# Attention: the low parts of a head's 1376 columns in one VectorE operation instead of a GpSimd and a VectorE operation

## The chip, the cores and the metric

The kernel runs on one core of a Trainium2 chip. The metric is the device time of one execution in microseconds. The engines are TensorE (PE for its matmuls, PEld for its weight loads), VectorE (DVE), ScalarE (ACT), GpSimd (POOL) and SyncE (SP), which issues the DMAs. Each engine runs its own instruction stream in order; they meet through semaphores.

## The reference

Two layers over 528 tokens (16 meta tokens and 512) of width 1024: a stick-breaking attention layer with a feed-forward part, then an RWKV-7 layer with a feed-forward part. The change lies in the attention, of which this is the core, for each of 16 heads of 64:

```python
z = jnp.einsum('bhtd,bhsd->bhts', qb, kb).astype(jnp.float32) * scale
mask = (s_idx[None, :] < t_idx[:, None]) & (s_idx[None, :] >= pad)
log_beta = jax.nn.log_sigmoid(z)
log_rest = jnp.where(mask, jax.nn.log_sigmoid(-z), 0.0)
later = lax.cumsum(log_rest, axis=3, reverse=True) - log_rest
att = jnp.where(mask, jnp.exp(log_beta + later), 0.0)
outs.append(jnp.einsum('bhts,bhsd->bhtd', att.astype(vb.dtype), vb))
```

The sum over later keys is taken by matmuls with a triangular matrix of ones.

## The kernel before

Everything is fp32. TensorE works on fp32r operands, so a factor that must keep its precision is split into two of them: a high part (a rounded copy, made by ScalarE) and a low part (the value minus its high part). A product then takes a matmul for each part: three for projections (`x_hi*w_hi`, `x_lo*w_hi`, `x_hi*w_lo`), two where the other factor is exact, as the matrix of ones is.

The attention goes through eight pairs of heads. The scores of one head lie in 1376 columns of 128 keys each: 512 columns in the first PSUM bank and 2 x 432 in the next two. `part(t, 0)` names the first 512 columns of a tile, `part(t, 1)` the other 864. The head `hp` = 0 of a pair has its scores in the PSUM tile `psg`, `hp` = 1 in `psx`.

For each head the steps are: VectorE clips the scores (`clip`, L408), ScalarE takes the exponential (L308) and the logarithm (L314), VectorE takes a maximum (`softplus`, L414), and `rest` is there. ScalarE makes its high part `rest_hi` (`rest_high`, L322), in two pieces of 512 and 864 columns. The low part `rest_lo` is made in two pieces too: GpSimd the first 512 columns (L538), VectorE the other 864 (`rest_low`, L419). With both, TensorE adds the sums within a block of keys (`own_block`, L627). VectorE adds up blocks of later keys (`later_keys`, L431), ScalarE makes their high part (`sums_high`, L330), VectorE the low part (`sums_low`, L436), and TensorE adds these (`later_blocks`, L638). ScalarE's exponential (L336) then gives the weights, with which TensorE multiplies the values (L660, L665).

Between these steps TensorE does the q, k and v projections of the next pair (`half`, L576), in pieces that the order written out in `tensor` puts between them. A projection needs its weights split into `w_hi` (ScalarE, L125) and `w_lo` (VectorE, L129). VectorE's order is also written out by hand: after `rest_low` of both heads come `later_keys` and `sums_low` of both, an eviction of a projection (L392), and then `unit_lo(3p + 4)`, the low part of the weights of the k projection, for which the TensorE block `half(3p + 4, 0)` waits. In the last pair there is no next projection, and the attention's output projection (L1219) fills in, in two pieces.

The semaphores of the change are `rlo_near` (raised by GpSimd's piece), `rlo_far` (raised by VectorE's piece) and `rhi_r` (raised by each piece of `rest_hi`, four times a pair). `own_block` waits for both of the first two, `later_keys` for `rlo_far` alone. `rest_low(p, 0)` stands between `softplus(p, 1, 0)` and `softplus(p, 1, 1)`.

Of the kernel before, what the change touches and what calls it, by code (L numbers as in the profile page):

```python
# [7 lines left out]
F32 = mybir.dt.float32  # L8
# [173 lines left out]
PAIRS = H // 2  # L182
# [9 lines left out]
class Attention:  # L192
# [175 lines left out]
    def vector(self, dve):  # L368
        k, b, nc = self.k, self.b, self.k.nc
# [46 lines left out]
        def rest_low(p, hp):  # L416
            n = 4 * p + 2 * hp + 1
            dve.wait_ge(self.rhi_r.h, n + 1)
            nc.vector.tensor_tensor(self.part(b.rest_lo[hp], 1), self.part(b.rest[hp], 1),  # L419
                                    self.part(b.rest_hi[hp], 1).bitcast(F32), ALU.subtract).then_inc(self.rlo_far.h, 1)  # L420

        def later_keys(p, hp):

# [36 lines left out]
        for p in range(PAIRS):  # L460
# [9 lines left out]
            evict(3 * p + 2, 1)  # L470
            softplus(p, 1, 0)
            rest_low(p, 0)
            softplus(p, 1, 1)
            rest_low(p, 1)
            later_keys(p, 0)
            later_keys(p, 1)
# [20 lines left out]
    def gpsimd(self, pool):  # L497
        k, b, nc = self.k, self.b, self.k.nc
        for c in k.psum_free:
            pool.sem_inc(c.h, c.start)  # L500
        nc.gpsimd.memset(k.ident[:], 0.0).then_inc(self.const_r.h, 1)
        nc.gpsimd.memset(k.ones[:], 1.0).then_inc(self.const_r.h, 1)
        nc.gpsimd.memset(k.eps[:, 0:1], RMS_EPS).then_inc(self.const_r.h, 1)
        nc.gpsimd.memset(k.eps[:, 1:2], 1.0).then_inc(self.const_r.h, 1)
        nc.gpsimd.memset(k.eps[:, 2:3], GN_EPS).then_inc(self.const_r.h, 1)
        pool.wait_ge(self.const_r.h, 5)
        nc.gpsimd.affine_select(out=k.ident[:], in_=k.ident[:], compare_op=ALU.not_equal, fill=1.0, base=0,
                                pattern=[[-1, P]], channel_multiplier=1).then_inc(self.const_r.h, 1)
        nc.gpsimd.memset(b.work[0][:], 0.0).then_inc(self.made_r.h, 1)
        nc.gpsimd.memset(b.work[1][:], -1.0).then_inc(self.made_r.h, 1)  # L510
        nc.gpsimd.memset(b.work[2][:], -1.0).then_inc(self.made_r.h, 1)
        nc.gpsimd.memset(b.vtok[:, 4, :], 0.0).then_inc(self.made_r.h, 1)
        nc.gpsimd.memset(b.kk[:, T:5 * P], 0.0).then_inc(self.made_r.h, 1)
        pool.wait_ge(self.made_r.h, 5)
        nc.gpsimd.affine_select(out=b.work[0][:], in_=b.work[0][:], compare_op=ALU.is_gt, fill=MASKED, base=0,
                                pattern=[[1, P]], channel_multiplier=-1).then_inc(self.made_r.h, 1)
        nc.gpsimd.affine_select(out=b.work[1][:], in_=b.work[1][:], compare_op=ALU.is_ge, fill=0.0, base=0,
                                pattern=[[-1, P]], channel_multiplier=1).then_inc(self.made_r.h, 1)
        pool.wait_ge(self.made_r.h, 7)
        pool.wait_ge(self.const_r.h, 6)  # L520
        for n in range(2):
            nc.gpsimd.tensor_copy(b.neg[:, n, :], b.work[0][:])
        nc.gpsimd.tensor_copy(b.tri[:], b.work[1][:])
        nc.gpsimd.tensor_copy(b.minus[:], b.work[2][:])
        nc.gpsimd.tensor_copy(b.ident_r[:], k.ident[:]).then_inc(self.made_r.h, 1)

        pool.wait_ge(self.sq_r.h, 2)
        nc.gpsimd.tensor_tensor(b.acc[:], b.sq[0][:], b.sq[1][:], ALU.add).then_inc(self.acc_r.h, 2)
        for m in range(2, KT - 1):
            pool.wait_ge(self.sq_r.h, m + 1)  # L530
            pool.wait_ge(self.acc_r.h, m)
            nc.gpsimd.tensor_tensor(b.acc[:], b.acc[:], b.sq[m % 2][:], ALU.add).then_inc(self.acc_r.h, 1)

        for p in range(PAIRS):
            for hp in range(2):
                n = 4 * p + 2 * hp
                pool.wait_ge(self.rhi_r.h, n + 1)
                nc.gpsimd.tensor_tensor(self.part(b.rest_lo[hp], 0), self.part(b.rest[hp], 0),  # L538
                                        self.part(b.rest_hi[hp], 0).bitcast(F32), ALU.subtract).then_inc(self.rlo_near.h, 1)

    def begin_out(self, pe, out, i):

        out.wait_weights(pe, i)
        for t in range(KT - 1):
            out.out_part(pe, i, t)
# [10 lines left out]
    def tensor(self, pe, out):  # L556
        k, b, nc = self.k, self.b, self.k.nc
# [62 lines left out]
        def own_block(p, hp):  # L620

            ps = (k.psg, k.psx)[hp]
            pe.wait_ge(self.rlo_near.h, 2 * p + hp + 1)
            pe.wait_ge(self.rlo_far.h, 2 * p + hp + 1)
            for bank, (at, end) in enumerate(zip(BANK_AT, BANK_AT[1:] + [SCORES])):
                for r in (b.rest_hi[hp], b.rest_lo[hp]):
                    mm(ps[:, bank, 0:end - at], b.tri[:], r[:, at:end], start=False, stop=True, skip_group_check=True)  # L627
# [79 lines left out]
        for p in range(PAIRS):  # L707
            fill = p < PAIRS - 1
            z(p)
            half(3 * p + 2, 0)  # L710
            half(3 * p + 2, 1)
            if fill:
                half(3 * p + 3, 0)
            else:
                pe.wait_ge(self.half_r.h, ATT_UNITS)
                self.wait_freed(pe, 3 * p + 2)
                self.begin_out(pe, out, 0)
            own_block(p, 0)
            if fill:
                half(3 * p + 3, 1, range(4))  # L720
            own_block(p, 1)
            if fill:
                half(3 * p + 3, 1, range(4, KT))
            later_blocks(p, 0)
            later_blocks(p, 1)
            if fill:
                half(3 * p + 4, 0, range(2))
            turn_v(p)
            if fill:
                half(3 * p + 4, 0, range(2, KT))  # L730
            else:
                pe.wait_ge(self.att_r.h, 4 * p + 4)
                self.begin_out(pe, out, 1)
            values(p)
            if fill:
                half(3 * p + 4, 1)
# [2049 lines left out]
```

## Time and profile before

| | |
|---|---|
| time, median of 3 runs | 1640.13 us (1637.53 to 1641.57) |
| the profiled execution's own time | 1632.62 us |
| its span | 1630.9 us |
| PE busy | 1562.1 us, 96% of the span |
| PEld busy | 1407.0 us, 86% |
| DVE busy | 835.9 us, 51% |
| ACT busy | 622.9 us, 38% |
| POOL busy | 156.3 us, 10% |
| attention's pairs of heads | from about 38 us to about 276 us of the span |

An engine's busy share says how full it is over the whole span; whether a longer instruction on it costs time depends on who waits for that instruction where it stands. Matmuls are pipelined and their ends are modelled, so the starts of TensorE's rows are the better measure. The mean granted clock of TensorE is 0.983 over the span. Times below are microseconds from the start of the span.

### The profile page before, as it was taken

How to read it: one execution, taken by the hardware profiler on the slowest of the kernel's cores; microseconds unless marked ns; L12 is line 12 of the kernel's file. 1: busy time of each engine (PE TensorE's matmuls, PEld its weight loads, DVE VectorE, ACT ScalarE, POOL GpSimd, SP SyncE). 2: the span in 40 equal slices, each digit the busy share in tenths (PEclk: the TensorE clock that was granted, in tenths of full speed). 3: DMA queues.
4: the chain of work that ended last, by engine and by line, in shares of the span. 5: the costliest groups of instructions: out<-in, count | busy, mean ns of one | idle time of the engine just before them, and what ended most of it. 6: DMA issues, size and time to landing. Idle time of an engine off the chain costs nothing. (4 is left out here: it accounts for less than half of the span.)

```text
span 1630.9 us, 35213 instructions
## 1 busy us (share of the span) xinstructions
PE 1562.1 (96%) x15881; PEld 1407.0 (86%) x15881; DVE 835.9 (51%) x1156; ACT 622.9 (38%) x847; POOL 156.3 (10%) x180
## 2 busy tenths in 40 slices
PE   7999998999999999979999979999789999999997
PEld 6989987999999999979998978888558888888886
DVE  5666765544433444367566545545575444244432
ACT  4655654422212222246567333333344222123322
POOL 3100100011000014000000321101010010001100
PEclk9999999999999999988999989999999999999999
DMA  4122121233332333242222100000313333233331
GB/s 133 53 72 59 53 72 58 80 94 89 104 90 78 91 91 111 74 138 70 74 73 59 39 19 4 4 4 4 107 39 91 90 98 107 88 88 98 101 95 64
DMA packets 214421, 120.63 MB, mean 74 GB/s; under 512 B 8728, under 2 KB 209584, under 8 KB 214016
## 3 DMA queue, kind: packets, MB, share of 16 engines
q1 hardware_dynamic: 213968, 118.31, 24.6%
q8 instruction: 125, 2.05, 0.5%
q14 instruction: 24, 0.20, 0.0%
q10 hardware_dynamic: 304, 0.08, 0.0%
HBM read 111.95 MB, written 6.42 MB: 73 GB/s over the span
## 5 line engine op out<-in xcount | busy, mean ns | idle before, releaser
L125 ACT ACTIVATE w_hi<-w_raw 128x1024 fp32r<-128x1024 f32 (+1 forms) x192 | 213.5, 1112 | 561.5 <-PE psg L785 461.5
L785 PE MATMUL psg<-x_hi,w_hi 128*128 128x264 f32 (+1 forms) x1080 | 350.8, 325 | 1.8 <-DVE w_lo L129 1.8
L785 PE MATMUL psg<-x_lo,w_hi 128*128 128x264 f32 (+1 forms) x1080 | 351.1, 325 | 0.0
L785 PE MATMUL psg<-x_hi,w_lo 128*128 128x264 f32 (+1 forms) x1080 | 350.3, 324 | 0.0
L129 DVE TENSOR_TENSOR w_lo<-w_raw,w_hi 128x1024 fp32r<-128x1024 f32 (+1 forms) x192 | 249.1, 1298 | 130.0 <-ACT w_hi L125 130.0
L785 PEld LDWEIGHTS psg<-x_hi,w_hi 128*128 128x128 f32 x1080 | 203.3, 188 | 20.3 <-DVE w_lo L129 2.2
L785 PEld LDWEIGHTS psg<-x_lo,w_hi 128*128 128x128 f32 x1080 | 203.1, 188 | 17.6 <-issue 0.2
L785 PEld LDWEIGHTS psg<-x_hi,w_lo 128*128 128x128 f32 x1080 | 203.7, 189 | 16.7
L785 PE MATMUL psg<-mid_hi,w_hi 128*128 128x264 f32 (+1 forms) x451 | 145.7, 323 | 0.0
L785 PE MATMUL psg<-mid_lo,w_hi 128*128 128x264 f32 (+1 forms) x451 | 145.6, 323 | 0.0
L785 PE MATMUL psg<-mid_hi,w_lo 128*128 128x264 f32 (+1 forms) x451 | 145.2, 322 | 0.0
L1867 PE MATMUL psg<-x_hi,w_hi 128*128 128x264 f32 x400 | 118.9, 297 | 9.5 <-DVE x_lo L1459 8.2
L959 DVE TENSOR_TENSOR res<-res,psg 128x512 f32<-128x512 f32 (+1 forms) x45 | 31.3, 695 | 173.3 <-PE psg L785 160.7
L1867 PE MATMUL psg<-x_hi,w_lo 128*128 128x264 f32 x400 | 116.7, 292 | 0.0
L1867 PE MATMUL psg<-x_lo,w_hi 128*128 128x264 f32 x400 | 116.6, 292 | 0.0
L1143 POOL TENSOR_TENSOR mid_lo<-up,mid_hi 128x528 fp32r<-128x528 f32 (+1 forms) x40 | 52.6, 1315 | 659.2 <-ACT mid_hi L908 659.2
L985 DVE TENSOR_TENSOR gate<-psg,rstd 128x528 f32<-128x528 f32 (+1 forms) x44 | 30.8, 700 | 122.4 <-PE psg L785 115.4
L1867 PEld LDWEIGHTS psg<-x_hi,w_hi 128*128 128x128 f32 x400 | 78.5, 196 | 14.8 <-issue 11.9
L785 PEld LDWEIGHTS psg<-mid_hi,w_hi 128*128 128x128 f32 x451 | 84.7, 188 | 6.9
L785 PEld LDWEIGHTS psg<-mid_hi,w_lo 128*128 128x128 f32 x451 | 84.8, 188 | 6.7
L785 PEld LDWEIGHTS psg<-mid_lo,w_hi 128*128 128x128 f32 x451 | 84.7, 188 | 6.7
L995 DVE TENSOR_TENSOR up<-psg,rstd 128x528 f32<-128x528 f32 (+1 forms) x44 | 30.8, 700 | 111.7 <-PE psg L785 111.7
(394 smaller groups left out, 3267.1 us busy)
## 6 DMA issues: line engine op xcount, KB each, us to landing
w_raw<-in_w_ffn_in_dram SPq DMA_DIRECT2D x88, 512.0 KB, 3.8
w_raw<-in_w_ffn_out_dram SPq DMA_DIRECT2D x32, 704.0 KB, 4.6
w_raw<-in_w_qkv_dram SPq DMA_DIRECT2D x24, 512.0 KB, 3.8
w_raw<-in_w_rkv_dram SPq DMA_DIRECT2D x24, 512.0 KB, 4.1
w_raw<-in_w_o_attn_dram SPq DMA_DIRECT2D x8, 512.0 KB, 4.0
w_raw<-in_w_o_rwkv_dram SPq DMA_DIRECT2D x8, 512.0 KB, 4.2
v_first<-v_pair SPq DMA_DIRECT2D x8, 264.0 KB, 2.0
res_kept<-res SPq DMA_DIRECT2D x1, 2112.0 KB, 7.8
```

What stands on the lines that cost most here:

```text
L125: k.nc.scalar.activation(k.w_hi[j][:, 0:kt, :], k.raw[j][:, 0:kt, :], ACT.Copy).then_inc(k.hi_ready[j].h, 1)
L129: k.nc.vector.tensor_tensor(k.w_lo[j][:, 0:kt, :], k.raw[j][:, 0:kt, :], k.w_hi[j][:, 0:kt, :].bitcast(F32), ALU.subtract).then_inc(k.lo_r ...
L785: done = k.nc.tensor.matmul(k.psg[:, 2 * j + c, 0:size], w[:, t, :], x, start=t == first and n == 0, stop=t == last and n == 2)
L959: nc.vector.tensor_tensor(row, row, self.psum(i % 2), ALU.add).then_inc(self.freed(i), 1)
L985: nc.vector.tensor_tensor(self.cols(b.gate), self.psum(0), self.cols(k.rstd), ALU.mult)\
L995: nc.vector.tensor_tensor(self.cols(b.up), self.psum(1), self.cols(k.rstd), ALU.mult)\
L1143: nc.gpsimd.tensor_tensor(b.mid_lo[:, r, self.t0:T], b.up[:, self.t0:T], b.mid_hi[:, r, self.t0:T].bitcast(F32), ALU.subtract).then_inc(se ...
L1867: done = nc.tensor.matmul(k.psg[:, 2 * j + c, 0:size], w[:, t, :], x[:, at:at + size], start=t == 0 and a == 0, stop=t == KT - 1 and a == 2)
```

## The change

VectorE makes the low parts of all 1376 columns of a head in one instruction. GpSimd's two instructions a pair are gone, and with them the semaphore wait of TensorE for them; the wait for `rlo_far` stays. The names `rlo_near` and its semaphore are left without use.

```diff
         def rest_low(p, hp):
             n = 4 * p + 2 * hp + 1
             dve.wait_ge(self.rhi_r.h, n + 1)
-            nc.vector.tensor_tensor(self.part(b.rest_lo[hp], 1), self.part(b.rest[hp], 1),
-                                    self.part(b.rest_hi[hp], 1).bitcast(F32), ALU.subtract).then_inc(self.rlo_far.h, 1)
+            nc.vector.tensor_tensor(b.rest_lo[hp][:], b.rest[hp][:], b.rest_hi[hp][:].bitcast(F32), ALU.subtract)\
+                .then_inc(self.rlo_far.h, 1)
...
-        for p in range(PAIRS):
-            for hp in range(2):
-                n = 4 * p + 2 * hp
-                pool.wait_ge(self.rhi_r.h, n + 1)
-                nc.gpsimd.tensor_tensor(self.part(b.rest_lo[hp], 0), self.part(b.rest[hp], 0),
-                                        self.part(b.rest_hi[hp], 0).bitcast(F32), ALU.subtract).then_inc(self.rlo_near.h, 1)
...
         def own_block(p, hp):

             ps = (k.psg, k.psx)[hp]
-            pe.wait_ge(self.rlo_near.h, 2 * p + hp + 1)
             pe.wait_ge(self.rlo_far.h, 2 * p + hp + 1)
```

On VectorE, in the first pair, the order of the instructions around the change is this (`rest_67`, `rest_hi_69`, `rest_lo_71` are those of head 0, `rest_68`, `rest_hi_70`, `rest_lo_72` those of head 1; what an instruction waits for stands in brackets):

```order
 L400 TENSOR_TENSOR v_pair<-psx,rstd 128x264 [waits unit_done0]
 L414 TENSOR_TENSOR rest_68<-rest_68,psx 128x512 [waits a_ln]
-L419 TENSOR_TENSOR rest_lo_71<-rest_67,rest_hi_69 128x864 [waits a_rest_hi]
+L419 TENSOR_TENSOR rest_lo_71<-rest_67,rest_hi_69 128x1376 [waits a_rest_hi]
 L414 TENSOR_TENSOR rest_68<-rest_68,psx 128x864 [waits a_ln]
-L419 TENSOR_TENSOR rest_lo_72<-rest_68,rest_hi_70 128x864 [waits a_rest_hi]
+L419 TENSOR_TENSOR rest_lo_72<-rest_68,rest_hi_70 128x1376 [waits a_rest_hi]
 L431 TENSOR_TENSOR rest_67<-rest_67 128x16 [waits a_lo_far]
 L431 TENSOR_TENSOR rest_67<-rest_67 128x144 [waits a_summed]
```

Nothing changes its place there; two instructions a pair grow from 864 to 1376 columns.

## Rows read from the trace of the kernel before

**Rows 1.** Windows view, one pair of heads: busy time and granted clock by engine.
```profile
core 0: us, PE busy (x) PEld busy (x) DVE busy (x) ACT busy (x) POOL busy (x), PEclk, DMA share, GB/s
128.00:158.00 30.00, 29.84 (x238) 27.16 (x237) 19.79 (x31) 16.82 (x23) 2.60 (x2) 1.00 0.21 63
```

**Rows 2.** Source view of L617, the last matmuls of a pair's scores.
```profile
L617 PE MATMUL psg<-neg,ident_r x8: 363/364/364, 38.0 to 248.0; 128*128 128x256 f32 x8
```

**Rows 3.** Waits of PE and PEld, 38 to 248 us: total, times, longest.
```profile
PE psg L576 <- DVE w_lo L129: 1.0, 6, 0.2
...
PEld psg L576 <- DVE w_lo L129: 1.7, 7, 0.3
```

**Rows 4.** Timeline of VectorE (DVE): start, duration, engine, line, [idle before <-releaser].
```profile
135.17 0.68 DVE L414 TENSOR_TENSOR rest<-rest,psx 128x512 f32<-128x512 f32 x1
135.84 1.06 DVE L419 TENSOR_TENSOR rest_lo<-rest,rest_hi 128x864 fp32r<-128x864 f32 x1
136.81 1.05 DVE L414 TENSOR_TENSOR rest<-rest,psx 128x864 f32<-128x864 f32 x1
138.86 1.06 DVE L419 TENSOR_TENSOR rest_lo<-rest,rest_hi 128x864 fp32r<-128x864 f32 x1 [0.99 <-ACT rest_hi L322]
139.83 1.90 DVE L431 TENSOR_TENSOR rest<-rest 128x16 f32<-128x16 f32 x6
141.81 2.03 DVE L436 TENSOR_TENSOR sum_lo<-rest,sum_hi 128x864 fp32r<-128x864 f32 x2
...
144.10 1.21 DVE L129 TENSOR_TENSOR w_lo<-w_raw,w_hi 128x1024 fp32r<-128x1024 f32 x1
```

**Rows 5.** Timeline of ScalarE (ACT), the same stretch.
```profile
134.90 0.91 ACT L322 ACTIVATE rest_hi<-rest 128x864 fp32r<-128x864 f32 x1
...
137.90 0.93 ACT L322 ACTIVATE rest_hi<-rest 128x864 fp32r<-128x864 f32 x1 [0.67 <-DVE rest L414]
140.85 1.83 ACT L330 ACTIVATE sum_hi<-rest 128x864 fp32r<-128x864 f32 x2 [2.03 <-DVE rest L431]
```

**Rows 6.** Timeline of GpSimd (POOL), the same stretch, second head.
```profile
137.31 1.30 POOL L538 TENSOR_TENSOR rest_lo<-rest,rest_hi 128x512 fp32r<-128x512 f32 x1 [2.36 <-ACT rest_hi L322]
```

**Rows 7.** Timeline of TensorE's weight loads (PEld), first load of four blocks.
```profile
137.40 0.19 PEld L627 LDWEIGHTS psg<-rest_hi,tri 128*128 128x128 f32 x1
...
140.12 0.19 PEld L627 LDWEIGHTS psx<-rest_hi,tri 128*128 128x128 f32 x1
...
142.93 0.19 PEld L638 LDWEIGHTS psg<-sum_hi,minus 128*128 128x128 f32 x1
...
145.37 0.19 PEld L576 LDWEIGHTS psg<-x_hi,w_hi 128*128 128x128 f32 x1 [0.25 <-DVE w_lo L129]
```

**Rows 8.** Groups of VectorE instructions by form: busy us, mean ns of one.
```profile
L129 DVE TENSOR_TENSOR w_lo<-w_raw,w_hi 128x1024 fp32r<-128x1024 f32 x160 | 196.9, 1231 | 105.3 <-ACT w_hi L125 105.3
L129 DVE TENSOR_TENSOR w_lo<-w_raw,w_hi 128x1408 fp32r<-128x1408 f32 x32 | 52.1, 1629 | 24.7 <-ACT w_hi L125 24.7
...
L419 DVE TENSOR_TENSOR rest_lo<-rest,rest_hi 128x864 fp32r<-128x864 f32 x16 | 16.9, 1058 | 7.9 <-ACT rest_hi L322 7.9
```

**Rows 9.** The view of rows 8, and the groups of GpSimd.
```profile
L378 DVE SCALAR_TENSOR_TENSOR x_lo<-res,vec,x_hi 128x528 fp32r<-128x528 f32 x8 | 8.9, 1131 | 0.0
L414 DVE TENSOR_TENSOR rest<-rest,psx 128x864 f32<-128x864 f32 x8 | 8.4, 1048 | 0.0
...
L408 DVE TENSOR_SCALAR rest<-psx 128x864 f32<-128x864 f32 x8 | 8.4, 1047 | 0.0
...
L943 DVE SCALAR_TENSOR_TENSOR x_lo<-res,vec,x_hi 128x528 fp32r<-128x528 f32 x8 | 6.1, 762 | 0.0
...
L532 POOL TENSOR_TENSOR x_acc<-x_acc,x_sq 128x528 f32<-128x528 f32 x5 | 8.7, 1732 | 2.0 <-ACT x_sq L296 1.4
```

**Rows 10.** Timelines of VectorE and of the weight loads, the last pair.
```profile
261.84 2.03 DVE L436 TENSOR_TENSOR sum_lo<-rest,sum_hi 128x864 fp32r<-128x864 f32 x2
...
262.95 0.19 PEld L638 LDWEIGHTS psg<-sum_hi,minus 128*128 128x128 f32 x1
```

## The prediction

> **What bounds the kernel now.** The windows view of one pair of heads comes first [rows 1]. In 30 us TensorE is busy 29.84 us, VectorE 19.79 us and GpSimd 2.60 us, at a granted clock of 1.00, the 2.4 GHz level. Read alone, this says that VectorE has a third of its time free and that two instructions there could grow at no cost. But a share tells nothing about place. The source view of L617, which a pair's scores end with, gives the period: eight starts from 38.0 to 248.0 us, so 210.0 / 7 = 30.0 us a pair [rows 2]. The question is then which wait TensorE ends last within a period. The view of waits has one releaser for its projections here, `w_lo` on VectorE (L129): seven times on the weight loads, 1.7 us in all, and six times on the matmuls, 1.0 us [rows 3]. The waits are small, some 0.24 us each, but they come once in each of the seven pairs that have a next projection. A wait that TensorE meets in every pair, however short, means that up to this point VectorE has no slack left: what VectorE gets later, TensorE gets later.
>
> So the last step is to follow VectorE back from that `w_lo`, by the timelines of one pair [rows 4, 5]. `w_lo` runs from 144.10 to 145.31, and TensorE's next load comes at 145.37, 0.06 us after it [rows 7]. In front of it on VectorE stand the two `sums_low` (141.81 to 143.84) and a short eviction, with no wait among them. The first `sums_low` starts as ScalarE's first `sums_high` ends (two of them take 1.83 us from 140.85, so the first ends near 141.77). That one waited for the third addition of `later_keys`, whose six additions run from 139.83 to 141.73, straight behind `rest_low` of head 1 (138.86 to 139.92). That waited 0.99 us for ScalarE's second piece of `rest_hi` (137.90 to 138.83). ScalarE had itself stood idle 0.67 us for `softplus` on VectorE (136.81 to 137.86), and this stood right behind `rest_low` of head 0 (135.84 to 136.90). The chain from 135.84 to 145.37 is therefore one of instructions that each start within 0.1 us of the end of another, with both `rest_low` in it. GpSimd's piece is not in it: it ends at 138.61, 1.31 us ahead of VectorE's piece of the same head [rows 6, 4].
>
> **The change, part by part.** *GpSimd's two instructions a pair go.* Worth nothing by themselves: TensorE waits for near and far together, and the far one came last, at 139.92 against 138.61 [rows 4, 6]. The second wait on TensorE goes with it; it had long been fulfilled. I take 0.
>
> *`rest_low` grows by 512 columns.* The trace has no 1376-column instruction, but it has the same operation on the same kinds of operands (SBUF twice, out in fp32r) at 864 columns with 1058 ns, at 1024 with 1231 ns and at 1408 with 1629 ns [rows 8]. Between the last two a column costs 398 / 384 = 1.036 ns. From 1408 down by 32 columns gives 1596 ns; from 864 up by 512 it gives 1588 ns. I take 1591 ns, so +0.533 us a head. The bounds: the same difference taken between 864 and 1408 gives 571 / 544 x 512 = 0.537 us. If the 512 columns brought a whole instruction's fixed part as well, 1058 - 864 x 1.036 = 163 ns, it would be 0.70 us a head. Below 0.53 no row leads.
>
> *Where it lands.* In head 0, +0.533 moves `softplus(p, 1, 1)`, then ScalarE's `rest_hi` and so the start of `rest_low` of head 1: the 0.99 us and 0.67 us of idle there do not absorb it, since each is a wait for the other engine of the same chain. In head 1 another +0.533 comes on top. From its end on, everything to `w_lo` is +1.066 us a pair. Nothing that TensorE does can absorb it, since TensorE is released by `w_lo`.
>
> *Where TensorE stands instead.* Its `own_block` of head 0 comes at 137.40 [rows 7]; the low part ends at 136.90 + 0.53 = 137.43, a wait of 0.1 us. `own_block` of head 1 comes at 140.12, and was ready at 139.92 + 0.06 = 139.98, so it had 0.14 us of slack. It is now ready at 139.98 + 1.07 = 141.05, and TensorE stands 0.93 us. `later_blocks` came at 142.93 [rows 7], 0.06 us after the first `sums_low` (141.81 + 1.06 = 142.87) [rows 4]: already set by VectorE, so 1.07 late. The wait for `w_lo` keeps its 0.2 us. So the loss is 1.07 us in each of seven pairs, of which 0.93 shows as a new wait at L627 for `rest_lo`, the rest at L638: 7 x 1.066 = 7.5 us.
>
> *The last pair.* Its two `own_block` lie together, after a piece of the output projection, and find their low parts there. `later_blocks` comes at 262.95, and its `sums_low` was done at 261.84 + 1.06 = 262.90 [rows 10]; 262.90 + 0.06 is the time at which it came, so the whole 1.07 us counts again. From there to the end of the attention all runs behind TensorE.
>
> *After the attention* nothing has changed, and all is moved by the sum. 7.5 + 1.07 = **8.5 us**. Against the profiled execution: 1632.6 + 8.5 = 1641.1 us, span 1639.4. That execution was 7.5 us below the median of the runs shown; on the median the same sum gives 1640.1 + 8.5 = **1648.6 us**.
>
> **Weighed against the skill.** GpSimd's piece could cost more than it seems, by slowing VectorE: VectorE's `x_lo` of 528 columns takes 1131 ns on average at L378, where GpSimd adds up squares for the same norm (L532), and 762 ns at L943, where it doesn't [rows 9]. The Trainium skill (SBUF — State Buffer, section "SBUF: two separate sides") says that a VectorE operation with two SBUF inputs and a GpSimd operation that reads SBUF shut each other out for a whole instruction. By that rule the pairs gain nothing from a free GpSimd, since `softplus` reads one input from PSUM and one from SBUF, and the sum stays at 8.5 us; the trace agrees with its 1048 ns. If the rule's lock held for `softplus` as well, the time would be that of rival 3.
>
> **The rivals.**
> 1. *Half of it is absorbed* (+4.3 us, 1644.4). The idle time of VectorE before `rest_low` of head 1, 0.99 us, is more than the 0.53 us that the first head adds [rows 4]. If that time were slack, only the second head's growth would reach TensorE: 8 x 0.533 = 4.3 us, 0.26%. Against it: ScalarE's idle 0.67 us in front of `rest_hi` ends with `softplus` [rows 5], which moves by the whole 0.53.
> 2. *More than the instructions* (+11 us and beyond). Either each grown instruction costs the 0.70 us bound, 16 x 0.70 = 11.2 us, 1651.3; or the new gap of 0.9 us on TensorE in each pair lowers the granted clock. Against the clock: it is 1.00 over the pair [rows 1], with its waits. If it fell to its 1.2 GHz level for 1 us of matmuls in each pair, that would add 1 us a pair, 1656.6.
> 3. *The freed port, and a faster kernel.* Place: VectorE's `softplus` beside GpSimd's piece, once a head. If each of them had been shut out up to the length of GpSimd's instruction, 1.30 us [rows 6], the change would give back 2.6 us a pair against 1.07 lost: 8 x (1.07 - 2.60) = -12.3 us, 1627.8. It decides from 1.07 us given back in a pair on. Against it: `softplus` of head 1 (136.81 to 137.86) lies half beside GpSimd (from 137.31) and takes 1048 ns, where the clip of the same width takes 1047 ns with GpSimd idle [rows 4, 6, 9].
> 4. *The share of VectorE is what counts, and nothing moves* (1640.1): VectorE has 10.2 us free in each pair [rows 1]. The waits for `w_lo` in all seven pairs speak against it [rows 3].
>
> **How the numbers follow.** A measurement of this kernel tells about 0.3%, 4.9 us, from no change. The forecast, a loss between 7.4 us (8 x 0.93, if only the new wait counted) and 9.5 us, has 0.83; a larger loss by rival 2 has 0.07. Rival 1 has 0.05, rival 4 has 0.03 and rival 3 has 0.02. So slower by over 0.3% is 0.90, within it 0.08, faster 0.02. The range reaches down to rival 1 with the scatter of the runs shown (1644.4 - 0.9 = 1643.5) and up to the 0.70 us bound with the same (1651.3 + 1.2 = 1652.5).
>
> **What would show it.** Right: `rest_low` at 128x1376 with 1591 ns; the starts of L617 some 31.07 us apart instead of 30.0; a new wait of TensorE at L627 for `rest_lo` on L419 of about 0.9 us, seven times, and none in the last pair; `w_lo` still the releaser at L576 with about 0.2 us; `softplus` unchanged at 1047 ns; the last matmul of the attention 8.5 us later, and everything after it as before. Wrong: a period of 30.5 us (rival 1), a granted clock below 1.00 between 38 and 285 us (rival 2), `softplus` clearly shorter (rival 3), or L627 without a wait (rival 4). The surest way to be wrong outside of this is a difference between executions in the 1350 us behind the attention, which the change does not touch.

## The result, and the profile after

The changed kernel's median was 1653.32 us over 8 executions (1643.94 to 1661.46), that of the kernel before 1641.46 us over 8. The ratio is 1.0073 with a 95% interval of 1.0045 to 1.0101: slower by 0.7%, 7 to 17 us. (A ratio here is not the quotient of the two medians beside it; three of the executions that follow, each over 1.5% above the fastest of its set, are in the medians and counts and are left out of ratios and means.) The forecast was slower by 8.5 us, 1648.6 us, in a range of 1643.5 to 1652.5 us. The direction was right and the size lies in the interval, but the median fell 0.8 us outside the range. The profiled execution took 1647.89 us, with a span of 1646.2 us, 15.3 us longer than that of before: 1.5 us of it lie ahead of the first pair's scores, 7.5 in seven pairs, 2.6 from the last pair's scores to the end of the output projection, and 3.6 behind it. So there are two questions: does the attention cost what the sum said, and where is the rest?

First the attention. The windows view of one pair, 31.07 us from scores to scores (busy time and count for each engine, granted clock, DMA), answers to [rows 1]:

```profile
core 0: us, PE busy (x) PEld busy (x) DVE busy (x) ACT busy (x) POOL busy (x), PEclk, DMA share, GB/s
132.72:163.79 31.07, 30.34 (x237) 27.25 (x237) 20.87 (x31) 16.82 (x23) 0.00 (x0) 1.00 0.20 60
```

TensorE's busy time rises by only 0.5 us of the 1.07 us, and VectorE's by 1.08 us. The source view of the last matmuls of the scores (now L610) gives the period, (257.0 - 39.5) / 7 = 31.07 us, against 30.0 in [rows 2]:

```profile
L610 PE MATMUL psg<-neg,ident_r x8: 364/364/364, 39.5 to 257.0; 128*128 128x256 f32 x8
```

The waits of TensorE and of its weight loads between 38 and 260 us (total, times, longest), against [rows 3]:

```profile
PE psx L619 <- DVE rest_lo L419: 4.0, 7, 0.6
PE psg L569 <- DVE w_lo L129: 1.1, 7, 0.2
...
PEld psx L619 <- DVE rest_lo L419: 5.5, 7, 0.8
...
PEld psg L569 <- DVE w_lo L129: 1.7, 7, 0.3
PEld psg L630 <- DVE sum_lo L436: 1.4, 7, 0.2
```

The wait for `w_lo` has stayed what it was, 1.7 us in seven times. In front of it stand two new ones: 5.5 us for `rest_lo`, seven times 0.79 us, and 1.4 us for `sum_lo`, seven times 0.2 us. In the last pair (the same view between 260 and 330 us) TensorE doesn't wait for `rest_lo`, as forecast, and the whole delay shows at `later_blocks`; the kernel before has no such wait there:

```profile
PEld psg L630 <- DVE sum_lo L436: 1.2, 1, 1.2
```

VectorE in the fourth pair, against [rows 4]:

```profile
140.58 1.59 DVE L419 TENSOR_TENSOR rest_lo<-rest,rest_hi 128x1376 fp32r<-128x1376 f32 x1
142.09 1.05 DVE L414 TENSOR_TENSOR rest<-rest,psx 128x864 f32<-128x864 f32 x1
144.13 1.59 DVE L419 TENSOR_TENSOR rest_lo<-rest,rest_hi 128x1376 fp32r<-128x1376 f32 x1 [0.99 <-ACT rest_hi L322]
145.64 1.90 DVE L431 TENSOR_TENSOR rest<-rest 128x16 f32<-128x16 f32 x6
147.62 2.03 DVE L436 TENSOR_TENSOR sum_lo<-rest,sum_hi 128x864 fp32r<-128x864 f32 x2
...
149.91 1.22 DVE L129 TENSOR_TENSOR w_lo<-w_raw,w_hi 128x1024 fp32r<-128x1024 f32 x1
```

ScalarE beside it, against [rows 5]:

```profile
143.17 0.93 ACT L322 ACTIVATE rest_hi<-rest 128x864 fp32r<-128x864 f32 x1 [1.20 <-DVE rest L414]
146.66 1.84 ACT L330 ACTIVATE sum_hi<-rest 128x864 fp32r<-128x864 f32 x2 [2.56 <-DVE rest L431]
```

And the first weight loads of three blocks, against [rows 7]:

```profile
145.78 0.19 PEld L619 LDWEIGHTS psx<-rest_hi,tri 128*128 128x128 f32 x1 [0.79 <-DVE rest_lo L419]
...
148.74 0.19 PEld L630 LDWEIGHTS psg<-sum_hi,minus 128*128 128x128 f32 x1 [0.21 <-DVE sum_lo L436]
...
151.18 0.19 PEld L569 LDWEIGHTS psg<-x_hi,w_hi 128*128 128x128 f32 x1 [0.24 <-DVE w_lo L129]
```

VectorE's idle time in front of the second `rest_low` is still 0.99 us: the first `rest_low` ended 0.53 us later, and with it the softplus, ScalarE's `rest_hi` (idle 1.20 us instead of 0.67) and the start of the second. From the end of the second on all is 1.07 us late. The groups by form (busy us, mean ns of one), against [rows 8, 9]:

```profile
L419 DVE TENSOR_TENSOR rest_lo<-rest,rest_hi 128x1376 fp32r<-128x1376 f32 x16 | 25.5, 1592 | 8.0 <-ACT rest_hi L322 7.9
...
L408 DVE TENSOR_SCALAR rest<-psx 128x864 f32<-128x864 f32 x8 | 8.4, 1048 | 0.0
...
L414 DVE TENSOR_TENSOR rest<-rest,psx 128x864 f32<-128x864 f32 x8 | 8.4, 1048 | 0.0
```

The operation of 1376 columns takes 1592 ns (forecast 1591), and the softplus still 1048 ns without GpSimd beside it.

### The profile page after: what moved, and what is told of

Its sections match the earlier page's. It is cut to its first block and busy times, and to the rows that moved or that the text cites. A ratio compares the mean times of both kernels' runs of the same rounds, so it can differ in the third digit from the quotient of the medians.

```text
span 1646.2 us, 35181 instructions
## 1 busy us (share of the span) xinstructions
PE 1570.2 (95%) x15881; PEld 1412.6 (86%) x15881; DVE 844.9 (51%) x1156; ACT 622.8 (38%) x847; POOL 134.0 (8%) x164
```

## The experiments

All kernels are compared with executions of the kernel before on the same chip. Besides the total, three things are read from each trace: the period of a pair; the **last pair**, from the start of the last scores' last matmul (the 248.0 of [rows 2]) to the start of a fixed matmul after the attention (at 314.9 us in the kernel before, the last that reads `o_hi` or `o_lo`); and a **stretch of the RWKV stage**, between the starts of two fixed matmuls, numbers 7400 and 14070 of the 15881 (counted from 0; 950.4 and 1207.8 us in the kernel before). No kernel here changes anything in that stretch.

| kernel | period, us | last pair | RWKV stretch | median (n) | before, same chip (n) | ratio, 95% interval |
|---|---|---|---|---|---|---|
| before | 30.01 | 66.92 | 257.4 | | | |
| changed | 31.08 | 69.55 | 262.4 | 1653.3 (8) | 1641.5 (8) | 1.0073, 1.0045 to 1.0101 |
| e1_again | 31.09 | 69.51 | 271.6 | 1659.0 (6) | 1643.9 (28) | 1.0107, 1.0075 to 1.0139 |
| e8_again2 | 31.07 | 69.53 | 261.2 | 1652.9 (11) | 1640.5 (34) | 1.0072, 1.0043 to 1.0102 |
| e11_again3 | 31.07 | 67.99 | 261.5 | 1651.9 (12) | 1643.0 (29) | 1.0052, 1.0029 to 1.0075 |
| e2_gaps | 30.0 | 68.43 | 260.4 | 1643.5 (12) | 1643.9 (28) | 1.0001, 0.9974 to 1.0029 |
| e3_head0 | 30.56 | 67.47 | 264.8 | 1649.2 (12) | 1643.9 (28) | 1.0033, 1.0011 to 1.0056 |
| e4_nopool | 30.01 | 66.93 | 261.8 | 1642.2 (12) | 1640.5 (34) | 1.0013, 0.9983 to 1.0042 |
| e5_once | 30.01 | 66.93 | 264.4 | 1650.8 (11) | 1643.9 (28) | 1.0065, 1.0033 to 1.0096 |
| e6_evict | 29.68 | 68.43 | 271.7 | 1638.1 (12) | 1640.5 (34) | 0.9989, 0.9963 to 1.0014 |
| e7_after_evict | 30.75 | 68.03 | 261.1 | 1647.4 (12) | 1640.5 (34) | 1.0036, 1.0007 to 1.0065 |
| e9_last | 30.01 | 67.99 | 264.4 | 1643.6 (12) | 1643.0 (29) | 1.0017, 0.9986 to 1.0047 |
| e10_notlast | 31.07 | 66.94 | 258.1 | 1652.8 (12) | 1643.0 (29) | 1.0070, 1.0040 to 1.0100 |

### Once more, and a delay in one piece (e1_again, e5_once)

The changed kernel was run again as it was:

> The changed kernel once more, unchanged, for the part of the result that the sum doesn't hold. Both theories: the period of a pair in the trace is 31.07 us against 30.0. Theory 1 (the change costs the 8.5 us of the attention, and the rest of the measured difference is scatter of the clock in the stages behind it): the median lies between 5 and 12 us above the kernel before on the same chip, and TensorE's time at its lower clock level comes in other places than in the first trace of the changed kernel. Theory 2 (the gaps in the attention make the clock fall more often behind it, a cost of its own of 3 to 4 us): again 11 to 13 us above, with a stretch at the lower level right behind the attention, near 291 us, as in the first trace.

Its median was 15.1 us above the kernel before, beyond both ranges, with only 6 executions (1655.3 to 1668.7). The period was as both said. A stretch of 3.4 us at the lower clock level came near 290 us again, as theory 2 had it; but the largest difference was in the RWKV stage. The windows view of that stretch, of the kernel before, of the changed kernel (with the time right behind its attention) and of this execution:

```profile
core 0: us, PE busy (x), PEclk, DMA share, GB/s
950.40:1207.80 257.40, 232.64 (x6684) 0.98 0.06 20
```

```profile
288.00:298.00 10.00, 8.26 (x55) 0.83 0.36 105
962.30:1224.70 262.40, 236.94 (x6682) 0.96 0.06 20
```

```profile
964.60:1236.20 271.60, 245.36 (x6687) 0.92 0.06 19
```

The same 6670 matmuls take 257.4 us at a granted clock of 0.98, 262.4 us at 0.96 and 271.6 us at 0.92, where 1.00 is 2.4 GHz and 0.5 is the lower level, 1.2 GHz. The kernel before had, in its one profiled execution, the least time of all thirteen traces.

In e5_once the loss was put in one piece ahead of the pairs:

```diff
         dve.wait_ge(self.rs_r.h, 2)
+        late = self.first_r
+        for n in range(7):
+            if n:
+                dve.wait_ge(late.h, n + 1)
+            nc.vector.tensor_tensor(b.rest[1][:, 0:2 * T], flat(k.res[:, 0:2, :]), flat(k.res[:, 2:4, :]), ALU.add)\
+                .then_inc(late.h, 1)
+        dve.wait_ge(late.h, 8)
         evict(0, 0)
```

> The kernel before with seven additions of 1056 columns on VectorE (unused results) in front of the first eviction of q: one delay of 8.3 to 8.9 us ahead of the attention's pairs instead of a small one in each pair. The pairs keep their period of 30.0 us. Theory 1 (scatter behind the attention): like the changed kernel, some 8.5 us more than before, and no difference between this kernel and the changed one that can be told. Theory 2 (the small gaps lower the clock later): 8.5 us here, and the changed kernel 3 to 4 us above it.

It missed in two ways. The seven additions came every 1.29 us, 9.0 us in all. And TensorE, which stood waiting for most of it, was at the lower level there, as the window shows (the same columns):

```profile
34.00:48.00 14.00, 4.10 (x16) 0.51 0.24 68
```

Up to 1073 us its trace runs about 11 us behind that of before; 9.0 of it is the additions, and 1.9 us arise between 34 and 37 us of the kernel before, in this window. Its median was 6.9 us above, its mean (1653.6 us) 10.3 us above that of all executions of the kernel before (1643.3 us). So it doesn't separate the theories as planned: it shows that the total of a kernel with a known delay scatters by some us around that delay.

### The same work in VectorE's waits (e2_gaps)

```diff
-        def rest_low(p, hp):
-            n = 4 * p + 2 * hp + 1
+        def rest_low(p, hp, which=1):
+            n = 4 * p + 2 * hp + which
...
             softplus(p, 0, 1)
+            rest_low(p, 0, 0)
             evict(3 * p + 2, 1)
             softplus(p, 1, 0)
             rest_low(p, 0)
             softplus(p, 1, 1)
+            rest_low(p, 1, 0)
             rest_low(p, 1)
```

`rest_low` handles the 512 or the 864 columns again, both on VectorE, and TensorE waits for both. GpSimd does nothing, as in the changed kernel.

> VectorE does all of the low parts as in the changed kernel, but the 512 columns of each head as an operation of their own, of some 0.69 us, in a place where VectorE waits anyway: in front of the second eviction of v (0.66 us idle) and behind the last softplus (0.99 us idle). Theory 1 (only the place on the chain to w_lo costs): a period of 30.0 us and the time of the kernel before, within 2 us. Rival (VectorE's added work costs wherever it stands): 2 x 0.6 us a pair, a period of 31.2 us and 9 to 10 us more than before.

VectorE in one pair:

```profile
139.19 1.04 DVE L414 TENSOR_TENSOR rest<-rest,psg 128x864 f32<-128x864 f32 x1
140.15 0.68 DVE L419 TENSOR_TENSOR rest_lo<-rest,rest_hi 128x512 fp32r<-128x512 f32 x1
140.90 0.43 DVE L400 TENSOR_TENSOR v_pair<-psx,rstd 128x264 f32<-128x264 f32 x1
...
141.92 1.06 DVE L419 TENSOR_TENSOR rest_lo<-rest,rest_hi 128x864 fp32r<-128x864 f32 x1
142.90 1.05 DVE L414 TENSOR_TENSOR rest<-rest,psx 128x864 f32<-128x864 f32 x1
143.86 0.68 DVE L419 TENSOR_TENSOR rest_lo<-rest,rest_hi 128x512 fp32r<-128x512 f32 x1
144.94 1.06 DVE L419 TENSOR_TENSOR rest_lo<-rest,rest_hi 128x864 fp32r<-128x864 f32 x1 [0.39 <-ACT rest_hi L322]
```

The two operations of 0.68 us lie in the gaps: the eviction at 140.90 comes as early after the softplus as before, and the idle time in front of the last `rest_low` has shrunk from 0.99 to 0.39 us. The period is 30.0 us and the ratio 1.0001. VectorE does more work here than in the changed kernel, 684 + 1058 - 1592 = 150 ns a head, and it costs nothing. The rival falls: the change's cost is where the work stands, not how much it is. (The edit splits the operation and moves one part of it; the two were not tried apart.) The average period over all pairs is 30.4 us only because the first pair ran at the lower level, as the windows show; from the second pair on there is no such stretch:

```profile
core 0: us, PE busy (x), PEclk, DMA share, GB/s
34.00:48.00 14.00, 13.19 (x60) 0.51 0.26 76
74.03:254.06 180.03, 179.08 (x1412) 1.00 0.21 63
```

### Head 0 alone (e3_head0)

```diff
+            whole = slice(0, SCORES) if hp == 0 else slice(512, SCORES)
+            nc.vector.tensor_tensor(b.rest_lo[hp][:, whole], b.rest[hp][:, whole],
+                                    b.rest_hi[hp][:, whole].bitcast(F32), ALU.subtract).then_inc(self.rlo_far.h, 1)
...
-            for hp in range(2):
+            for hp in (1,):
```

TensorE's wait for GpSimd's piece stays for head 1 alone.

> The change for head 0 alone; head 1 keeps GpSimd's piece. Theory 1 (the growth of head 0's operation passes through softplus and ScalarE's rest_hi undiminished): a period of 30.53 us, 4.3 us more than before, and TensorE waits some 0.4 us a pair at the second own_block. Rival 1 of the prediction (the 0.99 us idle before rest_low of head 1 absorbs it): a period of 30.0 us and no more time than before.

```profile
139.22 1.59 DVE L420 TENSOR_TENSOR rest_lo<-rest,rest_hi 128x1376 fp32r<-128x1376 f32 x1
140.73 1.05 DVE L414 TENSOR_TENSOR rest<-rest,psx 128x864 f32<-128x864 f32 x1
142.77 1.06 DVE L420 TENSOR_TENSOR rest_lo<-rest,rest_hi 128x864 fp32r<-128x864 f32 x1 [0.99 <-ACT rest_hi L322]
```

The 1.59 us of head 0 moves the softplus, and the 0.99 us idle in front of head 1's operation is undiminished. The period is 30.56 us, +0.55; the last pair +0.55. The median was 5.3 us above before. The prediction's first rival falls. TensorE's wait at the second `own_block` is 0.2 us, five times, in the view of its matmuls; its weight loads stand idle there 2.3 us in seven times, 0.33 us each, near the 0.4 us expected.

### GpSimd left out, VectorE as before (e4_nopool)

```diff
-        for p in range(PAIRS):
-            for hp in range(2):
-                n = 4 * p + 2 * hp
-                pool.wait_ge(self.rhi_r.h, n + 1)
-                nc.gpsimd.tensor_tensor(self.part(b.rest_lo[hp], 0), self.part(b.rest[hp], 0),
-                                        self.part(b.rest_hi[hp], 0).bitcast(F32), ALU.subtract).then_inc(self.rlo_near.h, 1)
+        pool.wait_ge(self.acc_r.h, KT - 1)
+        for hp in range(2):
+            nc.gpsimd.tensor_scalar(self.part(b.rest_lo[hp], 0), b.acc[:, 0:512].rearrange("p (a b) -> p a b", b=512), 0.0, None, ALU.mult)\
+                .then_inc(self.rlo_near.h, 1)
...
-            pe.wait_ge(self.rlo_near.h, 2 * p + hp + 1)
+            if p == 0:
+                pe.wait_ge(self.rlo_near.h, hp + 1)
```

> The kernel before without GpSimd's sixteen operations and without TensorE's wait for them; VectorE keeps its 864 columns. The low parts of each head's first 512 columns are left at zero, set once, so a part of the computation is missing. Theory 1 (GpSimd is off the path, TensorE waited for the far part): period 30.0 us, softplus of 864 columns still 1047 ns, the time of the kernel before within 2 us. Rival 3 of the prediction (GpSimd slows VectorE): a shorter softplus and a period of under 30.0 us.

```profile
L414 DVE TENSOR_TENSOR rest<-rest,psx 128x864 f32<-128x864 f32 x8 | 8.4, 1048 | 0.0
```

Softplus 1048 ns, period 30.01 us, ratio 1.0013 with 1 inside the interval. GpSimd's part was off the path and cost VectorE nothing; the third rival falls.

### An eviction moved into the gap (e6_evict, e7_after_evict)

```diff
             softplus(p, 1, 1)
+            if not last:
+                evict(3 * p + 3, 0)
             rest_low(p, 1)
...
             sums_low(p, 1)
-            if not last:
-                evict(3 * p + 3, 0)
             unit_lo(k, dve, 3 * p + 4, KT)
```

The same edit in the kernel before (e6_evict) and in the changed one (e7_after_evict).

> The kernel before with the eviction of q's first half (0.43 us) moved from in front of w_lo to in front of rest_low of head 1, where VectorE waits 0.99 us. Theory (w_lo is the last to release TensorE in every pair, by 0.24 us): TensorE's waits for w_lo at its projections vanish, the period falls from 30.00 to between 29.75 and 29.85 us, 1 to 2 us less in all, which the timed runs can't tell but the trace can. Rival (the wait for w_lo is only the last of many equal ones): the period stays at 30.0 us.

```profile
137.90 1.05 DVE L414 TENSOR_TENSOR rest<-rest,psx 128x864 f32<-128x864 f32 x1
138.87 0.43 DVE L392 SCALAR_TENSOR_TENSOR q_pair<-psg,rstd 128x264 f32<-128x264 f32 x1
139.95 1.06 DVE L419 TENSOR_TENSOR rest_lo<-rest,rest_hi 128x864 fp32r<-128x864 f32 x1 [0.65 <-ACT rest_hi L322]
...
142.90 2.03 DVE L436 TENSOR_TENSOR sum_lo<-rest,sum_hi 128x864 fp32r<-128x864 f32 x2
144.85 1.22 DVE L129 TENSOR_TENSOR w_lo<-w_raw,w_hi 128x1024 fp32r<-128x1024 f32 x1
```

The eviction lies at 138.87, in the gap, and `w_lo` follows the second `sums_low` directly. TensorE's waits for `w_lo` are gone, and the period is 29.68 us, 0.32 us less: that is nearly all of the 0.34 us that VectorE saves, and more than the 0.15 to 0.25 expected. Matmul for matmul against the kernel before, 0.30 us of it arises at the first one behind `w_lo`, so that wait cost a little more than the 0.24 us that the view of waits gives it. TensorE waits for no other engine in these seven pairs any more. Over seven pairs this is 2.3 us. The total can't show it: ratio 0.9989, 0.9963 to 1.0014. By the trace this is the best of the kernels here.

> The same move in the changed kernel. Theory: it takes 0.34 us off the way to w_lo, but the waits at own_block and at later_blocks stand, so the period falls from 31.07 to about 30.8 us: TensorE is held by later_blocks instead of w_lo, and the kernel is still some 6.8 us slower than before. Rival (only w_lo sets the period): 31.07 - 0.34 = 30.73 us, 6.1 us slower.

```profile
PEld psx L619 <- DVE rest_lo L419: 5.5, 7, 0.8
...
PEld psg L630 <- DVE sum_lo L436: 1.4, 7, 0.2
```

The period is 30.75 us, again 0.32 us less; TensorE's waits for `rest_lo` (5.5 us) and `sum_lo` (1.4 us) are as in the changed kernel, the one for `w_lo` is gone. 30.75 lies between the two figures and doesn't choose between them, but the waits do: `w_lo` holds TensorE no more, and `later_blocks` does, as the theory had it. Matmul for matmul against the kernel before, TensorE is 1.04 us late there and 0.76 us late behind `w_lo`. And between these two kernels the change costs 30.75 - 29.68 = 1.07 us a pair again, with no wait for `w_lo` in either: the growth reaches TensorE by `own_block` and `later_blocks` as well. A repair of one place gives back a third of the loss.

### The change in two halves, and more executions (e8_again2, e9_last, e10_notlast, e11_again3)

What was left was the excess over 8.5 us. In three of the first ten traces, all of the changed kernel, and in two others (e2_gaps, e6_evict) a stretch of 3.4 us at the lower level had come right behind the attention, which costs 1.5 us: it is the difference between 68.0 and 69.5 us in the column of the last pair. Theory 2 was that the changed last pair, with its new wait, brings it about.

> The changed kernel a third time, for more executions. Theory 1 (8.5 us in the attention, the rest is scatter of the clock): over all executions of the changed kernel the time at equal mean clock is 8 to 10 us above the kernel before, and this set lies between 6 and 12 us above. Theory 2 (a further cost of 3 to 4 us by a lower clock): this set is 11 us or more above, and its mean clock lies clearly below that of the kernel before, by 0.003.

Its median was 12.4 us above, just outside theory 1's window and inside theory 2's; its mean clock, 0.9769 against 0.9785 for the kernel before, is 0.0016 lower, not the 0.003 of theory 2. It settled nothing. The other half of theory 1, 8 to 10 us at equal mean clock over all executions, holds with 9.6 us (worked out below).

For the halves, the condition of e3_head0 was on the pair:

```diff
+            whole = slice(0, SCORES) if p == PAIRS - 1 else slice(512, SCORES)
```

and for e10_notlast `p < PAIRS - 1`, with GpSimd's loop and TensorE's wait for it on the other pairs.

> The change in the last pair alone; GpSimd keeps the other seven. Theory 1: 1.0 to 1.1 us more than before between the last pair's scores and the end of the output projection, at the full clock. Theory 2 (the longer gaps of TensorE in the changed last pair make the granted clock fall right behind the attention): besides, a stretch at the lower level near 285 us in its trace, which makes it 2.5 us, and a median 2 to 3 us above before.

> The change in the first seven pairs; the last pair keeps GpSimd's pieces. Theory 1: a period of 31.07 us, 7.5 us more than before, the last pair as before. Theory 2: no stretch at the lower level near 290 us, and 7.5 us in all, 3 to 4 us below the changed kernel.

> The changed kernel once more, on the same chip as the two halves of the change. Theory 1: the sum of the two halves, 8.5 us more than before at equal mean clock. Theory 2: a stretch at the lower level near 291 us again, and 11 us or more above before.

In the traces the halves add up: the last pair alone gives 67.99 us, +1.07, and the seven others 217.48 us instead of 210.04, +7.44, which is 8.5 us. Neither of these two traces has the stretch behind the attention, nor has e11_again3, the changed kernel's fourth trace, here with the RWKV stretch below it:

```profile
285.00:300.00 15.00, 11.69 (x103) 1.00 0.24 71
960.20:1221.80 261.60, 234.76 (x6687) 0.97 0.06 20
```

And its last pair is 67.99 us, as in e9_last. So the stretch comes without the change, and the change comes without it. It is there in 3 of the 6 traces with a wholly changed last pair (the changed kernel's four, e7_after_evict, e9_last), and in 2 of the 7 others; of the changed kernel alone it is 3 of 4. With such numbers it is not excluded that the change makes it likelier; its price is 1.5 us where it comes. The medians are less clean than the traces: e9_last was 0.6 us above before with 1.1 us in its attention, e10_notlast 9.8 with 7.4, and e11_again3 8.8 with 8.5.

## Why the prediction was right or wrong

**The sum.** Each step of it that the traces can check held. The operation of 1376 columns took 1592 ns, +0.534 us a head (forecast 0.533). The idle 0.99 us absorbed nothing, and the period rose by 1.07 us. The new wait of TensorE is at `own_block` of head 1, seven times 0.79 us of idle time; the delay there is larger, 0.92 us (forecast 0.93): the fourth pair begins 132.72 - 127.98 = 4.74 us later than before, so the load at 140.12 would have come at 144.86, and it came at 145.78. At `own_block` of head 0 the load came 0.09 us late (forecast 0.1). The wait for `w_lo` stayed 0.24 us. The last pair cost 1.07 us (67.99 against 66.92). GpSimd's part was worth 0 (e4_nopool). The shift of 8.5 us is measured in the traces: 7.45 to 7.5 us in the seven pairs, 1.07 us in the last. One reason was too narrow: nothing absorbs the growth "since TensorE is released by `w_lo`". e7_after_evict, in which `w_lo` holds nothing, loses the same 1.07 us against e6_evict, by `own_block` and `later_blocks`.

**What failed** is the last step, "on the median the same sum gives 1640.1 + 8.5", and with it the range's term "the scatter of the runs shown", 0.9 us below and 1.2 us above. The median of three executions was taken for that of the kernel. Over 89 later executions of the kernel before the median is 1642.4 us, and they reach from 1633.6 to 1658.7 us. And no row gives the 0.9 and the 1.2: the three runs shown reach 2.6 us below and 1.4 us above their median, and the prediction itself notes that the profiled execution lay 7.5 us below it. The end of the forecast interval, 9.5 us, isn't worked out either. The "surest way to be wrong", a difference between executions behind the attention, was named at the end of the prediction but had no share of the range.

The result lay 4.7 us above the forecast. The sum on the larger median is 1650.9 us, which answers for 2.2 us of it; the changed kernel's median over its 37 executions is 1653.4 us, and the other 2.5 us are the subject of the next part.

**Where the scatter comes from.** Every execution has a mean granted clock beside its time. Within each set of executions, 220 in all, a fitted line lets the time fall by 12.1 us for each 0.01 of mean clock, and with the clock taken out the standard deviation goes from 5.4 to 2.0 us. So most of it goes with TensorE's clock, and the traces show a stage in which it arises: the RWKV stretch, with the same matmuls, took from 257.4 to 271.7 us, and the time that TensorE spent at the lower level within it, from 6.8 to 41.0 us by the traces' clock records, goes with its length (correlation 0.92 over thirteen traces). Put to the same mean clock, 0.980, the means are 1641.5 us for the kernel before (89 executions), 1642.5 us for e2_gaps and e4_nopool (24), which have the same attention, and 1651.1 us for the changed kernel (37). The difference is 9.6 +- 0.9 us (95%) to the kernel before and 8.6 +- 1.1 us to the two others. Without that, the changed kernel's mean over its 37 executions is 11.0 us above the kernel before, with a 95% interval of 8.9 to 13.1 us (10.6 us, 8.4 to 12.8, over all 91 executions of before); its mean clock is 0.0011 lower, and whether by chance isn't known. That some 1 us more than the sum is a cost of the change is not shown, and not excluded. The method is too coarse for it: at equal clock e3_head0 lies 6.1 us above the kernel before with 4.4 us in its attention, and e6_evict 3.9 us below it with 2.3.

**The rivals.** Half absorbed: fell by e3_head0. The freed port: fell by e4_nopool and by the unchanged 1048 ns. Nothing moves, since VectorE has time free: fell, though e2_gaps shows its grain of truth, that free time can hold the work if it is in the right place. More than the instructions: the fixed part of a second instruction isn't there (1592 ns), and the clock in the pairs stayed at 1.00; a cost of the change behind the attention was not found beyond the 1 us just named.

## What to carry to other kernels

An engine that is busy for two thirds of a period can still have no slack: ask whether the bottleneck engine is released by it once in every period, and if so, follow the chain back from there. Every instruction in that chain passed its growth on in full here, while the same work cost nothing a few places away, in a wait for another engine. And where the program has stages in which TensorE's clock comes and goes, compare the same stretch of two traces, start to start; eight executions of each kernel told the sign of 0.5% but left its size between 7 and 17 us, and the range of a forecast needs a term for that scatter.

## What the runs showed of the hardware

The scatter itself was not expected: the same 6670 matmuls with their waits took 257.4 us in one execution and 271.7 us in another. The clock records of the thirteen traces hold two levels alone, 1.00 and 0.5. The lower one comes in stretches of 3.4 to 27.3 us, 47 to 94 us of a span in all.

A part of them has a fixed place. In every trace one of 10.2 to 17.1 us begins at matmul 5495, where TensorE has just waited 6.0 us, one of 10.2 us near matmul 5658, one of 6.8 us near 6710, and one of 6.8 or 13.7 us between 7456 and 7527. Others come in one execution and not in the next, behind the same wait: TensorE's first matmul on `k_pair` waits 2.6 us in all kernels but e5_once, and a stretch of 3.4 or 13.7 us begins there in 5 of these 12 traces; near matmul 2030, behind a wait of 1.7 us, it is 5 of 13. What makes the difference between such executions was not tried.

The lower level also stays while TensorE is busy: in e2_gaps, behind that wait for `k_pair`, the granted clock was 0.51 between 34 and 48 us, with 13.19 of 14 us busy.
